# Token-major projection loop written out, two projections ahead of the turns, with the index scores inside it

## The chip, the cores and the metric

One Trainium2 chip, one of its cores. The metric is the device time of the whole program in microseconds (us), the median of three runs.

## The reference

A two-layer decoder trunk over 1024 positions of width 1024, in float32. Layer 0 has a gated short convolution beside a sparse attention, layer 1 a spatial gating unit beside a chunked linear attention, and each layer ends in a gated convolutional FFN. The change concerns the front of the sparse attention in layer 0:

```python
p = h @ w_in                                   # h: rmsnorm of x
sc, q, k, v, iq, ik, iw = split(p)             # 8 heads of q, one k, one v, 4 index heads iq, one ik, 4 weights iw
q = rope(rmsnorm(q, q_g)); k = rope(rmsnorm(k, k_g)); iq = rope(iq); ik = rope(ik)
isc = relu(einsum('bqhd,bsd->bhqs', iq, ik))   # index scores, 4 heads
isc = einsum('bhqs,bqh->bqs', isc, iw * IDX_SCALE)
idx = top_k(causal(isc), 256)                  # per query
out = softmax(q . k[idx] * ATT_SCALE) @ v[idx] # per query, on the chosen keys
```

## The kernel before

The residual stream lies transposed in SBUF (`xT`, 128 rows of features by 1024 tokens, eight of them). Matmul operands are split into a high and a low float16 part and multiplied in three passes. Each engine has its own queue, written out by hand, and waits on counting semaphores; nothing but these queues and semaphores sets the order.

The stage in question handles eight blocks (`NB`) of 128 tokens, "token-major": tokens lie on the partitions.

- **Projection** (PE, `tm_project`, matmuls at L1218): 964 columns (q, k, v, iq, ik, iw), eight steps of depth 128, six matmuls each, into the pair of PSUM banks 0/1 or 2/3 by the block's parity. A pair is free once ACT has copied the block two back (`tm_copied`).
- **Copy** (ACT, `tm_copy`, L1438): the pair to `tm` in SBUF, unscaled.
- **Norm and rotation** (DVE, `tm_block`, L1942 to L1960): squares of q and k, their sum over each head (L1943), ACT's Sqrt of it (`tm_rms`, L1442), reciprocal, two multiplications over 576 columns, the rotation of q and k and then of iq and ik by four short operations each, the high and low part of v, the scaled index weights. Each operation waits for the one before by a semaphore.
- **Parts** (ACT `tm_hi`, L1451 to L1453; DVE `tm_lo`, L1966 to L1968): high and low float16 parts of all rotated heads, into `tm_split`.
- **Turn** (PE, `tm_turn`, L1229): sixteen transposes into banks 4 and 5. It waits for the low parts of its block and for both evictions of the turn before.
- **Eviction** (ACT `tm_evict`, L1458: q; DVE, L1972: iq and keys).

PE's order: projections 0 and 1 (with a turn of convolution vectors between them, which DVE scales in `conv_vectors`, L1854 and L1855, behind block 0), turn 0, then in a loop of three bodies projection 2, turn 1, projection 3, turn 2 and so on, last turn 7. So a projection stands between two turns, one block ahead. While block 0 is on DVE, POOL splits the first two weight units of the next section.

**Index scores** follow, once all evictions are done: for blocks 2 to 7 and four heads each, PE multiplies the block's iq with all keys up to the block's end (L1259, `L = 128 (b + 1)` columns, two passes, four pairs of banks in turn), ACT applies relu into one of two rows (L1487), DVE multiplies by the token's weight and sums the four heads in `score[b]` (L2000 for the first head, L2004 for the others). Blocks 0 and 1 need no scores.

**What follows.** PE projects the convolution mixer in twelve units (`ev_sc`, L890). Meanwhile ACT (L1509) and DVE (L2035, L2077, L2083) search each query's 256th score by 31 halvings; single operations of the convolution mixer (L2163 first) are laid in between, each waiting for its unit. The attention begins when the search ends. Output projection, FFN, layer 1 and its FFN follow on PE.

**Memory.** One large tensor, `arena`, holds what lives for a stage. `tw_hi` and `tw_lo`, the split weights of the projection, lie at word 9600 and 13456, `tm` and `tm_split` at 17312 and 21536, the scores at 8736 to 13344, so over `tw_hi`. Six of the eight raw weight rows are loaded by SP to 17312 and up and split by POOL (L757, L760).

Of the kernel before, what the change touches and what calls it, by code (L numbers as in the profile page):

```python
# [64 lines left out]
TM_STEPS = 15  # L65
# [27 lines left out]
def build(nc, t, out, stop=None):  # L93
    ctx = ExitStack()
    with ctx:
# [62 lines left out]
        rope_c = view(8736, [NB, ROT])  # L158
        rope_s = view(8864, [NB, ROT])
        qk_gain = view(8992, [NH_NORM * HD])  # L160
# [4 lines left out]
        sq9 = view(19752, [NH_NORM * HD])  # L165
        rot_a = view(20328, [NH_NORM, ROT])
        rot_b = view(20472, [NH_NORM, ROT])
        rms9 = view(20616, [2, 16])
# [5 lines left out]
        TW_RAW = [None, None] + [17312 + EV_TM * i for i in range(KT - 2)]  # L174
# [12 lines left out]
        relu_buf = att  # L187
# [624 lines left out]
        def _(pe):  # L812
# [391 lines left out]
            def tm_project(b, par, wait):  # L1204
                if wait is not None:
                    pe.wait_ge(tm_copied, wait)
                for k in range(KT):
                    if par == 0 and wait is None:
# [6 lines left out]
                    for a, w in ((h_hi, tw_hi), (h_hi, tw_lo), (h_lo, tw_hi)):  # L1215
                        lhs = a[:, k, bass.ds(b * P, P)]
# [3 lines left out]
                last.then_inc(tm_done, 1)  # L1220

            def tm_turn(par, made, evicted):

                pe.wait_ge(tm_low, made)
                if evicted is not None:
                    pe.wait_ge(tm_evict_act, evicted)
                    pe.wait_ge(tm_evict_dve, evicted)
                for j in range(16):
                    last = tr(ps[:, 4 + j // 8, :].bitcast(F16)[:, j % 8 * P:(j % 8 + 1) * P], tm_split[:, par, j, :],  # L1229
                              ident16[:])  # L1230
                last.then_inc(tm_turned, 1)

            tm_project(0, 0, None)
# [17 lines left out]
            pe.wait_ge(tm_evict_dve, NB)  # L1251
            for b in range(2, NB):
                L = P * (b + 1)
                for h in range(IH):
                    if b >= 3:
                        pe.wait_ge(relu_ready, IH * (b - 3) + h + 1)
                    for c in range(0, L, HALF):
                        for rows in (ik_hh, ik_ll):
                            last = mm(pair(h)[:, c:min(L, c + HALF)], iq_st[:, h, b * P:(b + 1) * P],  # L1259
                                      rows[:, c:min(L, c + HALF)], start=(rows is ik_hh), stop=(rows is ik_ll))  # L1260
                    last.then_inc(idx_done, 1)


# [87 lines left out]
        def _(act):  # L1351
            A = nc.scalar.activation

            def after_register_wait():
                act.sem_inc(act_passed, 1)
# [78 lines left out]
            def tm_copy(par, done, free):  # L1434
                act.wait_ge(tm_done, done)
                if free is not None:
                    act.wait_ge(tm_low, free)
                A(tm[:, par, :], pair(par)[:, 0:EV_TM], ACT.Copy, scale=W_UNSCALE).then_inc(tm_copied, 1)  # L1438

            def tm_rms(par, b1):  # L1440
# [4 lines left out]
            def tm_hi(par, roped, turned):  # L1445
                act.wait_ge(tm_roped, roped)
                if turned is not None:
                    act.wait_ge(tm_turned, turned)
# [1113 lines left out]
```

## Time and profile before

| what | value |
|---|---|
| median of three runs | 2339.06 us (2338.33 to 2340.55) |
| the profiled execution, whole | 2339.65 us |
| its span, first to last instruction | 2337.8 us |
| mean granted clock of TensorE over the span | 0.952 |
| PE, DVE, ACT, POOL busy | 92%, 56%, 40%, 47% |

A profile lists each instruction with its start and duration. "Idle before" is the time in which its engine had nothing to do ahead of it, and what released it. A granted clock of 1.00 is TensorE's full speed. Times in the section of rows are microseconds from the start of the span, mean durations of a group nanoseconds.

### The profile page before, as it was taken

To read this page: it belongs to the slowest core of one execution; us is meant where nothing else is said; L and a number is where in the kernel's file an instruction comes from. 1 tells how busy PE (TensorE), PEld (TensorE's weight loads), DVE (VectorE), ACT (ScalarE), POOL (GpSimd) and SP (SyncE) were. 2 spreads that over 40 slices of the span, in tenths; PEclk is the share of its full clock that TensorE was granted. 3 is DMA by queue.
4 is the path that set the end of the run, shared out by engine and by line. 5 is a ranking of instruction groups with operands and counts; after the bars stand their busy time and mean duration, and the time that the engine had idled before them with its cause. 6 is when DMAs were issued, how large, how long until landed. Compare 5 with 4: busy or idle time off the path is not lost. (4 is left out here: it accounts for less than half of the span.)

```text
span 2337.8 us, 29990 instructions
## 1 busy us (share of the span) xinstructions
PE 2140.0 (92%) x11534; PEld 1044.8 (45%) x11534; DVE 1298.5 (56%) x1979; ACT 936.3 (40%) x1361; POOL 1098.9 (47%) x729
## 2 busy tenths in 40 slices
PE   7779927889999999999989999779999999999998
PEld 3434415644434444444434444464444444444444
DVE  9778888843876147514644023785577416631652
ACT  5247866621553045304413221651355215521530
POOL 5103304214784667456586022013488457745642
PEclk8989969999999999999999999769899999999999
DMA  4001200001112112111132001001111211211112
GB/s 163 18 0 37 55 0 1 20 19 58 32 54 72 39 52 72 54 54 55 48 103 70 2 28 37 10 20 54 36 37 56 71 54 48 61 54 54 55 34 92
DMA packets 185984, 109.79 MB, mean 47 GB/s; under 512 B 3871, under 2 KB 180422, under 8 KB 185878
## 3 DMA queue, kind: packets, MB, share of 16 engines
q1 hardware_dynamic: 185414, 107.00, 15.7%
q0 software_dynamic: 464, 1.39, 0.2%
q8 instruction: 65, 1.06, 0.2%
q14 instruction: 41, 0.34, 0.0%
HBM read 104.18 MB, written 4.19 MB: 46 GB/s over the span
## 5 line engine op out<-in xcount | busy, mean ns | idle before, releaser
L626 POOL TENSOR_SCALAR w_scaled<-stage 128x1024 f32<-128x1024 f32 (+1 forms) x100 | 108.0, 1080 | 840.5 <-PE ps L890 530.8
L969 PE MATMUL ps<-h_hi,arena 128*128 128x512 f16 x1280 | 391.3, 381 | 10.8 <-DVE arena L2291 6.5
L890 PE MATMUL ps<-arena,w_hi 128*128 128x512 f16 x1504 | 388.2, 381 | 10.2 <-POOL w_lo L629 7.7
L969 PE MATMUL ps<-arena 128*128 128x512 f16 x1440 | 317.3, 379 | 0.1
L2247 DVE SCALAR_TENSOR_TENSOR xT<-ps,xT 128x1024 f32 (+1 forms) x64 | 78.3, 1224 | 409.4 <-PE ps L890 362.5
L969 PE MATMUL ps<-h_lo,arena 128*128 128x512 f16 x640 | 243.7, 381 | 0.0
L2300 DVE SCALAR_TENSOR_TENSOR work<-ps,fvec,work 128x1023 f32<-128x1023 f32 (+1 forms) x176 | 221.4, 1278 | 25.3 <-ACT work L1590 22.2
L890 PEld LDWEIGHTS ps<-arena,w_hi 128*128 128x128 f16 x1504 | 147.0, 98 | 191.0 <-POOL w_lo L629 11.1
L890 PE MATMUL ps<-arena,w_lo 128*128 128x512 f16 x752 | 224.6, 380 | 0.0
L969 PEld LDWEIGHTS ps<-arena 128*128 128x128 f16 x1440 | 140.8, 98 | 170.2 <-POOL arena L701 0.6
L969 PEld LDWEIGHTS ps<-h_hi,arena 128*128 128x128 f16 x1280 | 125.7, 98 | 165.5 <-issue 14.7
L629 POOL TENSOR_TENSOR w_lo<-w_scaled,w_hi 128x1024 f16<-128x1024 f32 (+1 forms) x92 | 188.7, 2051 | 7.7
L1590 ACT ACTIVATE work<-ps,fvec 128x1024 f32<-128x1024 f32 x88 | 105.1, 1201 | 196.1 <-DVE ps L2291 196.1
L1369 ACT ACTIVATE stage<-stage 128x2048 f32<-128x2048 f32 x36 | 68.7, 1909 | 215.8 <-DMA stage<-in_ffn_w_up_dram 215.8
L2310 DVE TENSOR_TENSOR work<-work 128x1024 f32<-128x1024 f32 x44 | 102.9, 2338 | 28.0 <-ACT work L1595 28.0
L1509 ACT ACTIVATE stat<-arena,srch 128x1024 f16<-128x1024 f32 (+1 forms) x124 | 113.9, 921 | 10.8 <-DVE srch L2068 10.2
L695 POOL TENSOR_TENSOR arena<-arena 128x1024 f16<-128x1024 f32 x40 | 116.9, 2922 | 0.0
L683 POOL TENSOR_TENSOR arena<-stage,arena 128x1024 f16<-128x1024 f32 x36 | 83.0, 2305 | 67.6 <-ACT arena L1388 67.6
L890 PEld LDWEIGHTS ps<-arena,w_lo 128*128 128x128 f16 x752 | 73.8, 98 | 89.4 <-issue 1.1
L2291 DVE TENSOR_TENSOR ps<-stat,ps 128x512 f32<-128x512 f32 x80 | 55.7, 696 | 104.1 <-PE ps L969 99.6
L890 PE MATMUL ps<-h_hi,w_hi 128*128 128x512 f16 x352 | 106.6, 385 | 5.3 <-ACT arena L1487 4.2
L890 PE MATMUL ps<-h_lo,w_hi 128*128 128x512 f16 x352 | 106.2, 384 | 0.0
(363 smaller groups left out, 3754.4 us busy)
## 6 DMA issues: line engine op xcount, KB each, us to landing
stage<-in_ffn_w_up_dram SPq DMA_DIRECT2D x76, 512.0 KB, 4.5
stage<-in_ffn_w_down_dram SPq DMA_DIRECT2D x32, 512.0 KB, 4.0
stage<-in_od_w_in_dram SPq DMA_DIRECT2D x20, 512.0 KB, 3.7
stage<-in_ev_w_in_dram SPq DMA_DIRECT2D x12, 512.0 KB, 3.7
arena<-in_ffn_w_up_dram SPq DMA_DIRECT2D x12, 512.0 KB, 5.0
stage<-in_ffn_w_down_dram SPq DMA_DIRECT2D x16, 384.0 KB, 3.4
arena<-in_x_dram SPq DMA_DIRECT2D x8, 512.0 KB, 7.8
stage<-in_ev_w_out_dram SPq DMA_DIRECT2D x8, 512.0 KB, 3.9
```

The lines of the kernel that those rows point to most:

```text
L626: nc.gpsimd.tensor_scalar(scaled, src, W_SCALE, 1.0, ALU.mult, ALU.mult).then_inc(w_parts, 1)
L629: nc.gpsimd.tensor_tensor(lo, scaled, hi, ALU.subtract).then_inc(w_split, 1)
L683: G.tensor_tensor(lo[:, 0:1024], raw_of(layer, f, 0), hi[:, 0:1024], ALU.subtract)
L695: G.tensor_tensor(lo[:, 2560:3584], sums_b.rearrange("p s c -> p (s c)"), hi[:, 2560:3584], ALU.subtract).then_inc(su_split, 1)
L890: last = mm(out2[:, hf * HALF:(hf + 1) * HALF], w, a[:, k0 + k, hf * HALF:(hf + 1) * HALF], start=(first and k == 0 and pss == 0), stop=(l ...
L969: last = mm(ps[:, bank, :], left, right[:, k, :], start=(fresh and k == 0 and pss == 0), stop=(k == 3 and pss == 2), skip_group_check=True)
L1369: A(raw_pair(layer, f), raw_pair(layer, f), ACT.Copy, scale=W_SCALE).then_inc(su_scaled, 1)
L1509: return A(signs[c - len(BY_DVE)], score[b][:], ACT.Sign, bias=srch[:, S_CAND, c:c + 1], accum_out=srch[:, S_COUNT, c:c + 1])
L1590: A(work[:, 2 * fi + g, :], pair(2 * fi + g), ACT.Identity, bias=fvec[:, layer, f + (6 + g) * FT:f + (6 + g) * FT + 1], scale=fvec[:, laye ...
L2247: V.scalar_tensor_tensor(out=xT[:, m, :], in0=pair(pair0 + step * mi), scalar=W_UNSCALE, in1=xT[:, m, :], op0=ALU.mult, op1=ALU.add).then_ ...
L2300: V.scalar_tensor_tensor(out=acc[:, s:], in0=y[:, 0:T - s], scalar=fvec[:, layer, tap:tap + 1], in1=acc[:, s:], op0=ALU.mult, op1=ALU.add) ...
L2310: V.tensor_tensor(work[:, 2 * fi + 1, :], work[:, 2 * fi, :], work[:, 2 * fi + 1, :], ALU.mult).then_inc(hid_f, 1)
```

## The change

- PE does projections 0, 1 and 2 before turn 0; from then on projection b stands ahead of turn b - 2. The loops on PE, ACT and DVE are written out.
- The index scores of block b are issued within the loop. The four heads of blocks 2, 3 and 4 stand behind steps 4 to 7 of projections 5, 6 and 7. Blocks 5 to 7 are mixed with turns 6 and 7 and follow them. ACT's relus and DVE's sums stand in their queues in matching places. They use banks 6 and 7 singly for blocks 2 and 3 and the pairs 6/7 and 0/1 by turns from block 4 on; the relu rows are the two rows of `stat`.
- Squares, the high part of v and the index weights are made by ACT from PSUM, ahead of its copy. DVE's three multiplications of the rotation of both groups stand first, then both sums; most waits between its operations are gone (`TM_STEPS` 5 for 15). `conv_vectors` stands behind the sum of squares of block 0.
- `tw_hi` and `tw_lo` move to 13344 and up, clear of the scores; `tm` and `tm_split` move to `work`; tables, `sq9`, `qk_gain` and six raw rows move within `arena`.

The diff, cut to its core:

```diff
-        tw_hi = view(9600, [KT, EV_TM], F16)
-        tw_lo = view(9600 + 3856, [KT, EV_TM], F16)
-        tm = view(17312, [2, EV_TM])
-        tm_split = view(21536, [2, 16, 2 * HD], F16)
+        tw_hi = view(13344, [KT, EV_TM], F16)
+        tw_lo = view(13344 + 3856, [KT, EV_TM], F16)
+        tm = work[:, 0:2, 0:EV_TM]
+        tm_split = work[:, 2:4, :].bitcast(F16).rearrange("p a (j c) -> p a j c", c=2 * HD)
-        TW_RAW = [None, None] + [17312 + EV_TM * i for i in range(KT - 2)]
+        TW_RAW = [None, None, 21056] + [8352 + EV_TM * i for i in range(KT - 3)]
-        relu_buf = att
+        relu_buf = stat
...
+            def index_head(b, h):
+                n = IH * (b - 2) + h
+                L = P * (b + 1)
+                if h == 0:
+                    pe.wait_ge(tm_evict_dve, b + 1)
+                if n >= 2:
+                    pe.wait_ge(relu_ready, n - 1)
+                if b < 4:
+                    dst = ps[:, 6 + h % 2, :]
+                else:
+                    dst = pair(3 if h % 2 == 0 else 0)
+                    if h == 1:
+                        pe.wait_ge(tm_copied, 7)
+                    if (b, h) == (4, 0):
+                        pe.wait_ge(relu_ready, n)
+                for c in range(0, L, HALF):
+                    for rows in (ik_hh, ik_ll):
+                        last = mm(dst[:, c:min(L, c + HALF)], iq_st[:, h, b * P:(b + 1) * P],
+                                  rows[:, c:min(L, c + HALF)], start=(rows is ik_hh), stop=(rows is ik_ll))
+                last.then_inc(idx_done, 1)
...
-            tm_project(1, 1, None)
+            tm_project(1)
+            tm_project(2)
             pe.wait_ge(vec_ready, 2)
-            tm_turn(0, 1, None)
+            tm_turn(0)
             wait_half(0, 1)
-            with pe.Fori(0, 3) as i:
-                tm_project(i * 2 + 2, 0, i * 2 + 1)
-                tm_turn(1, i * 2 + 2, i * 2 + 1)
-                tm_project(i * 2 + 3, 1, i * 2 + 2)
-                tm_turn(0, i * 2 + 3, i * 2 + 2)
-            tm_turn(1, 8, 7)
+            for b in range(3, NB):
+                tm_project(b, b - 3 if b >= 5 else None)
+                tm_turn(b - 2)
+            index_head(5, 0)
+            index_head(5, 1)
+            tm_turn(6)
+            index_head(5, 2)
+            index_head(5, 3)
+            index_head(6, 0)
+            tm_turn(7)
+            for h in range(1, IH):
+                index_head(6, h)
+            for h in range(IH):
+                index_head(7, h)
...
+            def tm_copy(b):
+                act.wait_ge(tm_done, b + 1)
+                if b >= 1:
+                    act.wait_ge(tm_step, TM_STEPS * (b - 1) + 1)
+                src = pair(b % 2)
+                A(sq9[:], src[:, 0:NH_NORM * HD], ACT.Square, scale=W_UNSCALE)
+                A(v_hi[:, b, :], src[:, V0:V0 + HD], ACT.Copy, scale=W_UNSCALE)
+                A(iw_tok[:, b, :], src[:, IW0:IW0 + IH], ACT.Copy, scale=W_UNSCALE * IDX_SCALE)
+                if b >= 2:
+                    act.wait_ge(tm_low, b - 1)
+                A(tm[:, b % 2, :], src[:, 0:EV_TM], ACT.Copy, scale=W_UNSCALE).then_inc(tm_copied, 1)
...
+            for b in range(NB):
+                tm_copy(b)
+                tm_rms(b)
+                if b >= 2:
+                    tm_evict(b - 2)
+                if b >= 4:
+                    relu(b - 2, 0, 1)
+                tm_hi(b)
+                if b == NB - 1:
+                    tm_evict(NB - 2)
+                if b >= 4:
+                    relu(b - 2, 2, 3)
+            relu(NB - 2, 0)
+            tm_evict(NB - 1)
+            relu(NB - 2, 1, 2, 3)
+            relu(NB - 1, 0, 1, 2, 3)
...
+            for b in range(NB):
+                tm_sum(b)
+                if b == 0:
+                    conv_vectors()
+                if b >= 2:
+                    tm_evict(b - 2)
+                tm_rotate(b)
+                if b == NB - 1:
+                    tm_evict(NB - 2)
+                if b >= 4:
+                    add_index(b - 2, 0)
+                tm_lo(b)
+                if b >= 4:
+                    add_index(b - 2, 1, 2, 3)
+            tm_evict(NB - 1)
+            for b in (NB - 2, NB - 1):
+                add_index(b, 0, 1, 2, 3)
```

`relu(b, *heads)` and `add_index(b, *heads)` are the former loops over heads as functions. `tm_sum` is the reduce of `sq9`, `tm_rotate` the rest of the former `tm_block`.

## Rows read from the trace of the kernel before

**Rows 1.** The page: span and section 1, busy time of each engine.

```profile
PE 2140.0 (92%) x11534; PEld 1044.8 (45%) x11534; DVE 1298.5 (56%) x1979; ACT 936.3 (40%) x1361; POOL 1098.9 (47%) x729
```

**Rows 2.** Windows by stretch: busy time of each engine, granted clock, DMA.

```profile
83.90:138.70 54.80, 53.35 (x306) 26.46 (x303) 39.24 (x100) 16.90 (x31) 0.00 (x0) 1.00 0.00 0
138.70:149.70 11.00, 1.07 (x16) 0.90 (x16) 7.84 (x20) 3.17 (x6) 0.00 (x0) 0.67 0.00 0
149.70:152.80 3.10, 1.89 (x16) 1.63 (x16) 0.69 (x1) 1.02 (x1) 0.00 (x0) 0.50 0.00 0
152.80:160.00 7.20, 7.03 (x32) 3.29 (x32) 4.92 (x8) 4.99 (x9) 0.00 (x0) 0.77 0.01 2
160.00:176.40 16.40, 10.65 (x48) 3.88 (x48) 14.07 (x16) 12.81 (x17) 0.00 (x0) 1.00 0.00 0
...
178.00:302.00 124.00, 124.00 (x571) 56.04 (x570) 106.72 (x467) 101.56 (x210) 44.33 (x30) 0.99 0.16 43
302.00:333.00 31.00, 1.22 (x7) 0.44 (x5) 25.75 (x112) 26.46 (x53) 0.00 (x0) 0.57 0.00 0
```

**Rows 3.** Timeline of PE, 290 to 345 us: the first scores of the attention.

```profile
327.97 0.61 PE L1282 MATMUL ps<-arena 128*128 128x128 f16 x4 [25.36 <-DVE work L2176]
```

**Rows 4.** Timeline of DVE: scores of the last block; first convolution product.

```profile
172.62 0.75 DVE L2000 TENSOR_SCALAR arena<-arena 128x1024 f32<-128x1024 f32 x1
173.85 4.06 DVE L2004 SCALAR_TENSOR_TENSOR arena<-arena 128x1024 f32<-128x1024 f32 x3 [0.49 <-ACT arena L1487]
...
202.43 1.22 DVE L2163 SCALAR_TENSOR_TENSOR work<-ps,work 128x1024 f32<-128x1024 f32 x1
```

**Rows 5.** Timeline of PE, 50 to 200 us: start, duration, instruction, idle before.

```profile
70.48 1.89 PE L1229 MATMUL ps<-ident,arena 128*128 128x128 f16 x16 [11.81 <-DVE fvec L1855]
...
83.85 0.98 PE L1218 MATMUL ps<-arena,h_hi 128*128 128x512 f16 x4
...
92.41 0.98 PE L1218 MATMUL ps<-arena,h_hi 128*128 128x512 f16 x4
...
138.74 1.07 PE L1229 MATMUL ps<-ident,arena 128*128 128x128 f16 x16 [0.34 <-DVE arena L1968]
149.73 1.89 PE L1229 MATMUL ps<-ident,arena 128*128 128x128 f16 x16 [9.92 <-DVE arena L1968]
...
176.44 0.92 PE L890 MATMUL ps<-h_hi,w_hi 128*128 128x512 f16 x2 [4.15 <-ACT arena L1487]
```

**Rows 6.** Timeline of DVE in block 0, beside POOL's splitting of weights.

```profile
58.87 2.11 DVE L1953 TENSOR_TENSOR arena<-arena 128x144 f32<-128x144 f32 x1
...
63.16 2.25 DVE L1956 TENSOR_TENSOR arena<-arena 128x144 f32<-128x144 f32 x1
```

**Rows 7.** Groups of instructions by line and shape, 84 to 178 us: mean ns.

```profile
L1458 ACT ACTIVATE arena<-ps 128x1024 f16 x6 | 6.1, 1013 | 0.0
L1438 ACT ACTIVATE arena<-ps 128x964 f32<-128x964 f32 x6 | 5.8, 973 | 11.0 <-PE ps L1218 8.1 <-DVE arena L1968 2.9
...
L1946 DVE TENSOR_TENSOR arena<-arena 128x576 f32<-128x576 f32 x6 | 4.5, 758 | 0.2
...
L1966 DVE TENSOR_TENSOR arena<-arena 128x512 f16<-128x512 f32 x6 | 4.2, 692 | 3.7 <-ACT arena L1453 3.7
L1972 DVE COPY arena<-ps 128x1024 f16 x6 | 4.1, 692 | 0.0
...
L2004 DVE SCALAR_TENSOR_TENSOR arena<-arena 128x896 f32<-128x896 f32 x3 | 3.5, 1152 | 0.6 <-ACT arena L1487 0.4
...
L1487 ACT ACTIVATE arena<-ps 128x640 f32<-128x640 f32 x4 | 2.7, 702 | 0.8 <-DVE arena L2004 0.6 <-PE ps L1259 0.3
...
L1442 ACT ACTIVATE arena<-small,eps 128x9 f32<-128x9 f32 x6 | 1.8, 304 | 9.7 <-DVE small L1943 9.7
```

**Rows 8.** The later line that alternates Square (L1772) with Sqrt.

```profile
L1776 ACT ACTIVATE gla_rms<-gla_rms,eps x4: 300/301/302, 1571.6 to 1582.7; 128x8 f32<-128x8 f32 x4
L1776 ACT ACT_TABLE_LOAD  x1: 1283/1283/1283, 1570.3 to 1570.3; - x1
```

More of the change, by code:

```diff
@@ L1202, in _, with tm_project @@
             spread(0)
-            def tm_project(b, par, wait):
-                if wait is not None:
-                    pe.wait_ge(tm_copied, wait)
+            def index_head(b, h):
[18 more added lines that the diff above has]
+                last.then_inc(idx_done, 1)
+            def tm_project(b, index=None):
+                par = b % 2
+                if b >= 2:
+                    pe.wait_ge(tm_copied, b - 1)
                 for k in range(KT):
-                    if par == 0 and wait is None:
+                    if b == 0:
                         wait_tile(0, 0, k)
@@ L1219, in tm_project, with tm_turn @@
                                       start=(k == 0 and a is h_hi and w is tw_hi), stop=(k == KT - 1 and a is h_lo))
[L1220 to L1227, printed above, removed]
+                    if k == KT - 1:
+                        last.then_inc(tm_done, 1)
+                    if index is not None and k >= KT - IH:
+                        index_head(index, k - (KT - IH))
+            def tm_turn(b):
+                pe.wait_ge(tm_low, b + 1)
+                if b:
+                    pe.wait_ge(tm_evict_act, b)
+                    pe.wait_ge(tm_evict_dve, b)
                 for j in range(16):
-                    last = tr(ps[:, 4 + j // 8, :].bitcast(F16)[:, j % 8 * P:(j % 8 + 1) * P], tm_split[:, par, j, :],
+                    last = tr(ps[:, 4 + j // 8, :].bitcast(F16)[:, j % 8 * P:(j % 8 + 1) * P], tm_split[:, b % 2, j, :],
                               ident16[:])
                 last.then_inc(tm_turned, 1)
-            tm_project(0, 0, None)
+            tm_project(0)
             pe.wait_ge(small_landed, 16 * 8)
@@ L1486, in _ @@
                         act.wait_ge(idx_added, n - 1)
[L1487 removed]
+                    src = ps[:, 6 + h % 2, :] if b < 4 else pair(3 if h % 2 == 0 else 0)
+                    A(relu_buf[:, n % 2, 0:L], src[:, 0:L], ACT.Relu).then_inc(relu_ready, 1)
+            for b in range(NB):
+                tm_copy(b)
+                tm_rms(b)
+                if b >= 2:
+                    tm_evict(b - 2)
[10 more added lines that the diff above has]
+            relu(NB - 1, 0, 1, 2, 3)
             A(small[:, 60:61], eps[:, 0:1], ACT.Copy).then_inc(a_cg, 1)
@@ L1947, in tm_block @@
+                st(V.reciprocal(rms9[:, b % 2, 0:9], rms9[:, b % 2, 0:9]))
+                st(V.tensor_tensor(heads, heads, rms9[:, b % 2, 0:9].unsqueeze(2).broadcast_to([P, 9, HD]), ALU.mult))
                 st(V.tensor_tensor(cur[:, 0:n9], cur[:, 0:n9], qk_gain[:], ALU.mult))
-                for c0, nh in ((Q0, 9), (IQ0, 5)):
+                groups = [(Q0, 0, NH_NORM), (IQ0, NH_NORM, IH + 1)]
+                for c0, r0, nh in groups:
                     g = cur[:, c0:c0 + nh * HD].rearrange("p (h d) -> p h d", d=HD)
+                    ra, rb = rot_a[:, r0:r0 + nh, :], rot_b[:, r0:r0 + nh, :]
@@ new lines, in tm_rotate @@
+                    V.tensor_tensor(rb[:, :, 0:8], g[:, :, 8:16], tab(rope_s, 0, 8), ALU.mult)
+                    last = V.tensor_tensor(rb[:, :, 8:16], g[:, :, 0:8], tab(rope_s, 8, 16), ALU.mult)
+                st(last)
+                for c0, r0, nh in groups:
+                    g = cur[:, c0:c0 + nh * HD].rearrange("p (h d) -> p h d", d=HD)
+                    V.tensor_tensor(g[:, :, 0:16], rot_a[:, r0:r0 + nh, :], rot_b[:, r0:r0 + nh, :], ALU.add)
+                V.tensor_tensor(v_lo[:, b, :], cur[:, V0:V0 + HD], v_hi[:, b, :], ALU.subtract).then_inc(tm_roped, 1)
```

139 lines of the change are left out of this document (42 added, 97 removed).

## The prediction

> **What bounds the kernel now.** The page says PE is busy for 92% of the span [rows 1], an average that says nothing of the stage the change touches. So I read the first 333 us stretch by stretch, in the windows [rows 2]. From 83.9 to 138.7 us PE does five projections and works nearly all the time. From 138.7 to 152.8 it works 3 us of 14. From 152.8 to 176.4 come the index scores; PE works 18 of 24 us, DVE 19. From 178 to 302 PE projects the convolution mixer without a gap, DVE and ACT search for the top keys. From 302 to 333 PE is idle for all but 1.2 us and the search still runs: the attention starts when the search ends, and PE's wait of 25.36 us there is for DVE [rows 3]. The search starts when the last index score is summed, at 177.91 us [rows 4]. So one moment sets all that follows: the end of the last sum. Whatever it gains, the attention gains.
>
> Which wait comes last ahead of it? PE's timeline [rows 5] shows three. PE stands 11.81 us before the turn of block 0, as DVE finishes that block late: beside POOL's splitting of weights, operations of DVE that take 0.3 us in later blocks take 2.11 and 2.25 us [rows 6]. PE stands 9.92 us before the turn of block 7, as no projection is left to lay over that block's chain. And only then do the index scores begin.
>
> **Part by part.** Durations are those of [rows 7] unless another group is named. I lay the new order out by hand on three queues, with 0.05 to 0.1 us for each semaphore.
>
> *Two projections ahead of the turn.* Block 0's chain on DVE keeps its start, since POOL's splits stay where they are. It loses the square (0.76 us), the cast and the scaling, but DVE now turns the convolution vectors in front of the rotation (0.8 us) and still meets POOL. I get it rotated at 66.8 us and its low part done at 69.5, against 69.7 before. PE has projection 2 to do meanwhile (58.6 to 68.4), so it waits 1.2 us in place of 11.81. Turn 0 ends at 70.5 and projection 3 starts there; ACT's copy of block 1, which it needs, ends at 69.9. Before, it started at 83.85 [rows 5]. **Gain 13.3 us.**
>
> *Projections 3 to 7.* The eight steps of a projection start 1.223 us apart (83.85 to 92.41 in seven [rows 5]), so 9.8 us; a turn takes 0.9 us of PE. Five projections and turns 1 to 4 are 52.5 us. New inside projections 5 to 7 are the twelve heads of index blocks 2 to 4: 8 x (384 + 512 + 640) columns at 1.223/2892 us make 5.2 us, and 0.6 us for their starts. Turn 1 waits 0.3 us for ACT's eviction of block 0, queued behind the copy of block 2. Together 58.7 us, so turn 5 starts at 129.2. Before, turn 6 stood in that place, 54.9 us after the start of projection 3 [rows 5]. **Loss 3.8 us.**
>
> Does the ACT-DVE chain keep up? For a block that carries heads it is: copy with Square and two small copies, reduce 0.75, DVE's eviction 0.69, reciprocal to low part of v 3.9 (two multiplications of 0.76, six small ones, three sums, no waits between those), then ACT's parts 1.25 once its relus of two heads are done, DVE's parts 1.4, one sum, one relu, next copy. ACT's new work is unseen. Square of 576 columns from PSUM lies under the relu of 640 (0.70) and above one of 384 (0.49); I take 0.68. The small copies lie under the 0.30 of the 9-element Sqrt; I take 0.25 and 0.20. With the copy (0.97) that is 1.85 us, against 0.97. The chain comes to 12 us a block, PE's cycle to 12.2, 12.6 and 13.2. The first head of each block finds its keys evicted 1.5 to 2.5 us early. With 0.95, 0.30 and 0.25 the end is 1.5 us later; with 0.50, 0.20 and 0.15 it is 0.7 us earlier.
>
> *The tail.* ACT's copy of block 7 stands behind the relu of index block 4, head 3, and ends at 132.4 instead of 131. Reduce, eviction of block 5 (133.9), rotation to 137.8, eviction of block 6, first sum of index block 5, low part to 140.6. Then DVE is nearly always at work: three sums of 1.02 us and their waits (to 143.8), eviction of block 7 and the first sum of block 6 (145.1), a wait of 0.6 us for ACT's relu, three sums of 1.15 (149.2), and for block 7 what it takes today, 5.3 us (172.62 to 177.91 [rows 4]). The last sum ends at 154.4, 25.3 us after turn 5; before it ended 39.2 us after turn 6. **Gain 13.9 us.** Sum: 13.3 - 3.8 + 13.9 = 23.4 us.
>
> *The clock.* In the stretches where PE worked 1 of 11 and 1.9 of 3.1 us, the granted clock was 0.67 and 0.50, so at the lower level (1.2 GHz) for much or all of them; it was 0.77 in the next 7 us, and 1.00 from 160 us on with PE busy for 65% [rows 2]. The new tail leaves PE two holes of 4 and 3 us, at 130 and 137.5, so some heads will run at 1.2 GHz. If all of blocks 5 to 7 did, a head's matmuls and relu, with two pairs of banks to alternate between and not four, would take over from DVE as the limit: end at 158.6, 4.2 us later. From the rows I allow a quarter, 1.1 us. **Net gain 22.3 us.**
>
> *Costed at nothing.* The parts, tables and weights in other rows: the same eight loads on SP's queue in the same order, nothing moved past another; the rope tables wait for POOL's first split, which the first projection needs as well. Loops written out: five projections and turns of 9.8 and 0.9 us fill 53.5 of the 54.8 us of their window [rows 2], so the branches and waits they hold cost at most 0.3 us a block. No DMA and no POOL work is added; POOL's splits and SP's loads of the next section wait for PE's units and shift with them. The relu rows now lie where ACT writes its signs, but those wait for the search, after the last sum. PE's convolution section starts at the last relu, 1.6 us before the last sum, as today, so its lead over the search stays. After the search everything waits on other engines, none on a fixed time; the shift goes through whole.
>
> *A rule against it.* ACT now alternates Square, Copy and Relu with Sqrt, eight times. In the later line that alternates four groups of Squares with four Sqrts, one table load of 1.28 us stands before the first Sqrt and none before the others [rows 8]; so none here. The Trainium skill (ScalarE: Activation LUTs, Table sets: the hidden batching unit) says functions in different sets cost a load at each switch, and names copy and relu, not Square, among those in every set. By that reading this would be two loads a block; the row speaks against it, and by the row the sum stays.
>
> **The rivals.** (a) *The clock holds the tail down*: 4.2 us lost, 2339.1 - 19.2 = 2319.9. For it: 0.50 at 150 us. Against: 1.00 at 65% load. (b) *Table loads*: 2 x 1.28 us on ACT for blocks 1 to 7. Laid out, projection 7 ends 4.7 us later and the last sum at 161.2: 2322.3. (c) *Lockstep, slower than before*: ACT stands for head 1 in front of its parts, head 1 stands in the second half of a projection, and that projection waits for ACT's copy two blocks back. If these lock, blocks 5 to 7 pay one after another: PE's 13.2 plus the chain's 12, 25 us, against 12.7. That is 37 us more: 2354. It turns slower than before from 20 us a block on. Against: each wait reaches one block further back than the lock needs. (d) *Nothing arrives*: the search's end is held by something else, or the search slows by what was gained. The first convolution product in the search, at 202.4 us [rows 4], needs PE's second unit, due two units of 10.3 us (124/12) and a slow first 2.3 us after 176.4: a cover of 3 us. But both shift together: 2339.
>
> **The numbers.** The sum is made against the profiled execution: 2339.65 us, of which 2337.8 are the span and 1.85 lie around it and stay. 2339.65 - 22.3 = 2317.4; it lies 0.6 above the median of the runs, 2339.06, so the median should come to 2316.8. Chances: forecast 0.68, (a) 0.16, (b) 0.04, (c) 0.04, (d) 0.03, and 0.05 for a chain that is longer without locking (up to 2330). The unknown costs give 2315 (short ACT work, no cold clock) to 2321 (long ACT work, rival a). The clock's phase at later stage starts moves by the shift, an estimate of 2 us either way from the 3 us that stretches at 0.77 and 0.50 lose here. So 2312 to 2325. A measurement of this kernel tells about 0.2%, 4.7 us, from no change. Faster by more than that: 0.68 + 0.16 + 0.04 + 0.05 = 0.93; within: 0.03; slower: 0.04.
>
> **What would show it.** Right: PE's wait before the turn of block 0 near 1 us; projection 3 starts near 70.5; turn 5 near 129; the last sum near 155.5; the convolution section still 124 us; PE's wait before the attention still 25 us. Wrong: table loads between Sqrt and Square; heads inside projections that wait for evictions or relus by more than 1 us; blocks 5 to 7 longer than 14 us; a granted clock near 0.5 from 140 to 155; a stage after the search with another length than before.

## The result, and the profile after

The changed kernel takes 2311.94 us (median of 4 runs, 2310.62 to 2315.07); the kernel before, measured beside it, 2339.56 us (2338.33 to 2340.55). The ratio is 0.9887 with a 95% interval of 0.9875 to 0.9898: 27.6 us less, where 22.3 were forecast. The median lies 0.06 us below the lower end of the predicted range; those of two repeats below, 2314.21 and 2312.97, lie inside it. The profiled execution has a span of 2310.9 us against 2337.8, so 26.9 us less.

The page after, where [rows 1] was read before. PE's share is the same 92% and its busy time fell by 12.6 us, so 14.3 of the 26.9 us are idle time that went. The matmuls are the same 11534, and the mean granted clock rose from 0.952 to 0.958:

```profile
PE 2127.4 (92%) x11534; PEld 1037.7 (45%) x11534; DVE 1286.1 (56%) x1955; ACT 940.6 (41%) x1385; POOL 1098.9 (48%) x729
```

Windows of the changed kernel, for [rows 2] (columns: the stretch, its length, then the busy time of PE, PEld, DVE, ACT and POOL, the granted clock, the DMA share and GB/s):

```profile
69.40:127.10 57.70, 57.70 (x339) 29.69 (x337) 39.75 (x110) 27.66 (x60) 0.00 (x0) 1.00 0.00 1
127.10:134.00 6.90, 3.43 (x27) 1.98 (x25) 6.14 (x13) 4.32 (x8) 0.00 (x0) 0.77 0.01 2
134.00:138.10 4.10, 2.57 (x27) 1.76 (x26) 3.66 (x12) 3.55 (x6) 0.00 (x0) 0.97 0.00 0
138.10:150.10 12.00, 8.49 (x48) 3.40 (x48) 10.50 (x11) 9.26 (x11) 0.00 (x0) 1.00 0.00 1
150.10:154.00 3.90, 3.86 (x18) 1.79 (x19) 3.49 (x14) 0.00 (x0) 0.00 (x0) 1.00 0.00 0
...
274.20:304.30 30.10, 0.42 (x2) 0.00 (x0) 24.42 (x106) 26.36 (x56) 0.00 (x0) 0.56 0.00 1
```

From 69.4 to 127.1 us PE has no idle time at all: five projections with twelve heads in them. The stretch with 1 us of work in 11 is gone; what is left of it are the 6.9 us from 127.1, with the clock at 0.77. After 134 us the clock is 0.97 to 1.00.

PE's timeline of the changed kernel, for [rows 5] and [rows 3] (start, duration, instruction, in brackets the idle time before it and what ended it):

```profile
68.46 1.05 PE L1255 MATMUL ps<-ident,work 128*128 128x128 f16 x16 [0.79 <-DVE work L2004]
69.35 0.98 PE L1241 MATMUL ps<-arena,h_hi 128*128 128x512 f16 x4
...
127.06 1.06 PE L1255 MATMUL ps<-ident,work 128*128 128x128 f16 x16
...
131.59 2.74 PE L1222 MATMUL ps<-arena 128*128 128x512 f16 x8 [3.47 <-DVE arena L2008]
...
138.06 0.92 PE L1222 MATMUL ps<-arena 128*128 128x512 f16 x4 [1.53 <-ACT stat L1498]
...
150.14 0.59 PE L890 MATMUL ps<-h_hi,w_hi 128*128 128x512 f16 x2 [1.69 <-ACT small L1519]
...
304.34 0.61 PE L1305 MATMUL ps<-arena 128*128 128x128 f16 x4 [29.73 <-DVE work L2211]
```

Turn 0 waits 0.79 us instead of 11.81, and projection 3 begins 14.50 us earlier. Turn 5 (127.06) takes the place of turn 6 before (138.74). The last row is the surprise: the attention begins 23.6 us earlier, but PE's wait ahead of it has grown from 25.36 to 29.73 us. The convolution section, which starts at 150.14, gained 26.3 us, and the search that runs beside it gained less.

DVE's timeline of the changed kernel, for [rows 4] and [rows 6], and then what follows the last sum:

```profile
58.56 2.12 DVE L1988 TENSOR_TENSOR arena<-work,arena 128x144 f32<-128x144 f32 x1
...
62.87 2.14 DVE L1990 TENSOR_TENSOR arena<-work,arena 128x40 f32<-128x40 f32 x1
...
146.16 0.75 DVE L2017 TENSOR_SCALAR arena<-stat,arena 128x1024 f32<-128x1024 f32 x1
147.39 4.06 DVE L2021 SCALAR_TENSOR_TENSOR arena<-stat,arena 128x1024 f32<-128x1024 f32 x3 [0.48 <-ACT stat L1498]
...
160.16 6.01 DVE L2087 TENSOR_SCALAR work<-srch 128x6 int32<-128x6 int32 x31
166.20 0.22 DVE L2112 TENSOR_SCALAR srch<-srch 128x1 int32<-128x1 f32 x2
```

The last sum ends at 151.45 (147.39 + 4.06), 26.46 us earlier than before. Ahead of the search DVE makes a table of flipped bits, 31 short operations on six elements. DVE's timeline of the kernel before shows what they took there:

```profile
186.63 2.35 DVE L2052 TENSOR_SCALAR work<-srch 128x6 int32<-128x6 int32 x31
189.00 0.22 DVE L2077 TENSOR_SCALAR srch<-srch 128x1 int32<-128x1 f32 x2
```

They took 2.35 us, and now take 6.01. The search's first bit therefore starts 22.80 us earlier (189.00 to 166.20): 3.66 of the 26.46 us were given back in one place. POOL's timeline names the other party. The first row is of the kernel before:

```profile
188.94 1.04 POOL L626 TENSOR_SCALAR w_scaled<-stage 128x1024 f32<-128x1024 f32 x1 [123.69 <-PE ps L890]
```

and these are of the changed kernel:

```profile
160.95 1.09 POOL L626 TENSOR_SCALAR w_scaled<-stage 128x1024 f32<-128x1024 f32 x1 [95.99 <-PE ps L890]
162.00 1.04 POOL L627 TENSOR_SCALAR w_hi<-stage 128x1024 f16<-128x1024 f32 x1
163.13 2.15 POOL L629 TENSOR_TENSOR w_lo<-w_scaled,w_hi 128x1024 f16<-128x1024 f32 x1
```

POOL splits weights of the convolution section as soon as PE's first unit releases their buffer. Before, that unit began with the clock at 0.57, as a window of the kernel before shows:

```profile
176.40:180.40 4.00, 3.96 (x11) 1.53 (x12) 3.55 (x15) 0.00 (x0) 0.00 (x0) 0.57 0.00 0
```

It took 12.5 us to POOL's start, and POOL began as the flips ended (188.94 against 188.98). Now PE begins the unit at full clock, POOL starts 10.81 us after it, and its three operations (4.33 us) lie inside the flips. The Trainium skill (SBUF — State Buffer, Who interferes with whom) says that VectorE and GpSimd share one pair of ports as an exclusive lock, that a VectorE operation with two inputs in SBUF contends for it with a GpSimd instruction that reads SBUF, and so does a `tensor_scalar` in a two-port form, where the loser stands for the whole instruction. The rows agree in the times: 3.66 us are lost over 4.33 us of POOL, and in block 0 an operation that takes 0.31 us in later blocks takes 2.12 and ends at 60.68, where POOL's subtraction ends at 60.52. Which form the flips take, no row shows.

ACT's timeline of the changed kernel, the table load of block 0 and then block 5, for the prices taken by estimate and for [rows 8]:

```profile
54.09 1.28 ACT L1471 ACT_TABLE_LOAD   x1
...
102.93 0.65 ACT L1462 ACTIVATE arena<-ps 128x576 f32<-128x576 f32 x1
103.46 0.23 ACT L1463 ACTIVATE arena<-ps 128x64 f16<-128x64 f32 x1
103.56 0.20 ACT L1464 ACTIVATE arena<-ps 128x4 f32<-128x4 f32 x1
103.61 1.01 ACT L1467 ACTIVATE work<-ps 128x964 f32<-128x964 f32 x1
105.44 0.30 ACT L1471 ACTIVATE arena<-small,eps 128x9 f32<-128x9 f32 x1 [0.82 <-DVE small L1962]
```

This table load stands before the first Sqrt, and none follows in the seven blocks after it.

### The profile page after: what moved, and what is told of

It reads as the page before. It is cut to its first block and busy times, and to the rows that moved or that the text cites. A ratio compares the mean times of both kernels' runs of the same rounds, so it can differ in the third digit from the quotient of the medians.

```text
span 2310.9 us, 29711 instructions
## 1 busy us (share of the span) xinstructions
PE 2127.4 (92%) x11534; PEld 1037.7 (45%) x11534; DVE 1286.1 (56%) x1955; ACT 940.6 (41%) x1385; POOL 1098.9 (48%) x729
## 5 line engine op out<-in xcount | busy, mean ns | idle before, releaser
L969 PE MATMUL ps<-h_hi,arena 128*128 128x512 f16 x1280 | 391.3, 381 | 11.6 <-DVE arena L2326 6.5
L2335 DVE SCALAR_TENSOR_TENSOR work<-ps,fvec,work 128x1023 f32<-128x1023 f32 (+1 forms) x176 | 221.4, 1278 | 26.5 <-ACT work L1619 23.4
L1585 ACT ACTIVATE work<-xT 128x1024 f32 (+1 forms) x24 | 25.4, 1057 | 201.5 <-DVE xT L2282 201.5
```

The lines of the kernel that those rows point to most:

```text
L969: last = mm(ps[:, bank, :], left, right[:, k, :], start=(fresh and k == 0 and pss == 0), stop=(k == 3 and pss == 2), skip_group_check=True)
L2335: V.scalar_tensor_tensor(out=acc[:, s:], in0=y[:, 0:T - s], scalar=fvec[:, layer, tap:tap + 1], in1=acc[:, s:], op0=ALU.mult, op1=ALU.add) ...
```

## The experiments

The first set was measured against 13 runs of the kernel before, 2338.94 us in the median. The question: which part of the change brings which part of the 26.5 us at the last sum, and does POOL cause the 3.7 us lost behind it?

**The index heads back behind the loop.** The second projection ahead stays; the relus and sums follow the heads, on four pairs of banks.

```diff
             for b in range(3, NB):
-                tm_project(b, b - 3 if b >= 5 else None)
+                tm_project(b)
                 tm_turn(b - 2)
...
             tm_turn(6)
...
             tm_turn(7)
...
+            pe.wait_ge(tm_evict_act, NB)
+            pe.wait_ge(tm_evict_dve, NB)
+            for b in range(2, NB):
+                for h in range(IH):
+                    index_head(b, h)
```

> The changed kernel with all index scores behind the loop again, on four pairs of banks as in the kernel before; two projections ahead and ACT's squares stay. My theory (each part is worth what it takes off the way to the last index sum): without heads the five projections and turns run at 10.7 us a block, turn 7 starts near 131, and the 25.1 us of index scores of the kernel before follow, so the last sum is near 158, 7 us later than in the changed kernel: 2319 us, give or take 2. Rival (DVE has the same number of sums to do either way, so hiding them in the loop brings nothing): last sum within 2 us of 151.5, 2312. Rival (the heads inside cost PE more than they save): below 2310.

Measured: 2321.53 us (2318.34 to 2323.68), ratio 0.9925 (0.9909 to 0.9942); the last sum at 159.78, 8.3 us later than in the changed kernel. PE's timeline of this kernel:

```profile
126.32 1.05 PE L1246 MATMUL ps<-ident,work 128*128 128x128 f16 x16 [2.98 <-ACT arena L1474]
...
131.64 1.89 PE L1246 MATMUL ps<-ident,work 128*128 128x128 f16 x16 [4.26 <-DVE work L1985]
134.64 7.14 PE L1213 MATMUL ps<-arena 128*128 128x384 f16 x32 [1.12 <-ACT arena L1474]
...
158.46 0.77 PE L890 MATMUL ps<-h_hi,w_hi 128*128 128x512 f16 x2 [4.31 <-ACT small L1500]
```

The holes before turns 6 and 7 (2.98 and 4.26 us) stay empty, and all heads come after them. Two more things can be read. PE's convolution section starts after a wait of 4.31 us, its first pair of matmuls takes 0.77 us instead of 0.59, POOL starts 12.50 us behind it instead of 10.81, and DVE's flips take 2.34 us: with the longer hole the collision is gone. And the span, 2319.9, is 9.0 us above that of the changed kernel, although the attention starts only 5.7 us later (310.02); the rest comes at later stage starts.

**One projection ahead as well.** The kernel above, with turn b - 1 behind projection b as in the kernel before; the evictions on ACT and DVE move with the turns. What is left of the change are the squares and small copies on ACT, the shorter rotation with fewer waits, the written-out loops and the new rows.

```diff
-            tm_project(2)
...
-            for b in range(3, NB):
+            for b in range(2, NB):
                 tm_project(b)
-                tm_turn(b - 2)
-            tm_turn(6)
+                tm_turn(b - 1)
```

> As the run with the index scores behind the loop, and also one projection ahead of the turn, as in the kernel before; what is left of the change is ACT's squares, the fewer waits on DVE and the other rows. My theory: turn 0 near 68, block time 10.7 us in place of 11.1, block 7's chain 9 us in place of 11, last sum near 170, 8 us before that of the kernel before: 2331 us. So the second projection ahead is worth 12 us, the index scores inside 7, the rest 8. Rival (the lighter operations of DVE carry the change, two ahead only moves the wait): under 2320. Rival (they carry nothing): 2338 or more.

Measured: 2333.6 us (2331.38 to 2337.98), ratio 0.9978 (0.9969 to 0.9988); the last sum at 172.03. PE's timeline of this kernel:

```profile
69.00 1.87 PE L1246 MATMUL ps<-ident,work 128*128 128x128 f16 x16 [11.28 <-DVE work L1982]
...
143.86 1.89 PE L1246 MATMUL ps<-ident,work 128*128 128x128 f16 x16 [8.16 <-DVE work L1982]
```

Both long holes are back: 11.28 us before turn 0, 8.16 before turn 7. The last sum now has its parts: 177.91 before, 172.03 with the lighter block (5.9 us), 159.78 with a second projection ahead (12.3), 151.45 with the heads inside (8.3). The expectation had named 8, 12 and 7 for them. Each is larger by itself than the 4.7 us that a measurement tells from no change, and the whole kernel's times are in the same order (2339, 2334, 2322, 2312). They were taken off in this one order only, so what each would bring without the others is not shown.

**The squares back on DVE.** ACT loses the Square, DVE gets a multiplication of 576 columns per block.

```diff
-                A(sq9[:], src[:, 0:NH_NORM * HD], ACT.Square, scale=W_UNSCALE)
...
+                V.tensor_tensor(sq9[:], qk, qk, ALU.mult).then_inc(tm_step, 1)
```

> The changed kernel with the squares of q and k on DVE again (from the copied row, with a wait before the reduce). My theory: in the blocks of the loop PE is the limit and hides 0.3 us of a longer chain; only block 0 and the tail show it, last sum 0.3 to 1 us later, 2312 to 2313 us, no change that can be measured. Rival (the chain of ACT and DVE sets the block): 0.3 to 0.8 us in each of seven blocks, last sum 2 to 5 us later, 2314 to 2317.

Measured: 2314.98 us (2313.82 to 2317.07), ratio 0.9897 (0.9881 to 0.9914). Turns 0 to 5 start within 0.08 us of the changed kernel's, the first head of block 5 at 131.91 instead of 131.59, and the last sum at 152.58, 1.1 us later (the two repeats below, at 151.57 and 151.06, lie 1.0 and 1.5 us ahead of it). So inside the loop PE sets the pace and either engine may square; in the tail DVE does, and the multiplication costs there. The change of the total lies inside the spread of runs.

**POOL waits for the flips.** One wait before POOL's split for the third unit, for a semaphore that reaches 2 only when the flips are done.

```diff
-            split_section("ev_sc", 6, 2, peeled=6)
+            split_section("ev_sc", 6, 2, peeled=6, after_two=lambda: pool.wait_ge(cand_ready, 2))
```

> The changed kernel; POOL holds its split of the third unit of the convolution section until DVE has written the 31 flip rows ahead of the search (6.0 us in the changed kernel, 2.35 before). My theory (the flips met POOL's split, and POOL held DVE up): the flips take 2.4 us again, the search starts 3.7 us earlier, PE waits under 1 us for the third unit, and the end comes 2.5 to 4 us earlier, 2308 to 2309.5 us, apart from 2 us either way by the clock. Rival (the flips are slow for another reason, such as where they lie): they stay at 6 us and the time stays at 2312. Rival (PE then waits for POOL's late unit and the search meets that): the section of PE grows by 4 us and the time stays or grows.

Measured: 2310.97 us (2307.81 to 2313.08), ratio 0.9885 (0.9868 to 0.9901), profiled span 2306.0. DVE's timeline of this kernel, the flips:

```profile
159.21 2.34 DVE L2087 TENSOR_SCALAR work<-srch 128x6 int32<-128x6 int32 x31
```

and PE's, the start of the attention:

```profile
299.05 0.61 PE L1305 MATMUL ps<-arena 128*128 128x128 f16 x4 [25.38 <-DVE work L2211]
```

The flips take 2.34 us again, PE's wait before the attention is 25.38 us as before ([rows 3]: 25.36), and the attention begins 28.9 us earlier than before instead of 23.6. Of the 5.3 us between them, 0.95 lie ahead of the last sum (150.50), where the edit changes nothing. The last sum to the attention takes 148.55 us against 152.89: 3.67 of these 4.34 us are the flips, the other 0.67 stand in the search behind them. Keeping POOL away is the only difference, so POOL's splits are shown as the cause of what the search lost. In the median of the runs the gain is smaller than in the span (1 us, across two sets of measurements), and by the total alone it would not be shown.

The second set (before: 2339.22 us) repeats the changed kernel and asks three things: how far two profiles of one kernel differ, whether the meeting with POOL depends on the clock, and what POOL costs in block 0.

**The changed kernel again**, without an edit.

> The changed kernel once more, for a second profiled execution and beside the next runs. My theory on the 3.3 us that the first profile gained behind the search (PE's stage starts met another phase of the clock): last index sum again 26 to 27 us ahead of the kernel before, flips again 6 us, and the shift behind the search between 22 and 28 us, not steady at 27: it moves by 1 to 3 us at 360 to 390 us and at 1640 to 1740 us. Time 2310 to 2315. Rival (something in the change speeds the later stages): the same 3.3 us at the same places.

Measured: 2314.21 us (2311.46 to 2315.02), ratio 0.9888 (0.9872 to 0.9905). Last sum 151.57, flips 6.03 us, attention at 304.45: the same to 0.12 us. But the output projection behind the attention starts at 468.05, where the first profile has 466.42, and the span is 2311.8. So 1.6 us of the first profile's lead at that place are not the change's.

**A delay of 0.9 us in the tail.**

```diff
             for b in (NB - 2, NB - 1):
+                if b == NB - 1:
+                    for _ in range(1):
+                        V.memset(work[:, 3, :], 0.0)
                 add_index(b, 0, 1, 2, 3)
```

> The changed kernel with one write of 1024 columns of zeros on DVE between index blocks 6 and 7, nothing else: everything behind it is put off by that time, about 0.6 to 1 us. My theory (what follows the last sum is rigid apart from the clock and the meeting of POOL with the flips): last sum 0.6 to 1 us later, flips still near 6 us, time 1 us more, give or take 2. Rival (the flips' meeting is a matter of a fraction of a us): flips change by over 1 us.

Measured: 2315.41 us (2314.35 to 2316.12), ratio 0.9894 (0.9878 to 0.9911). The last sum ends at 152.86, 1.4 us later (0.45 of them stand already at turn 0, ahead of the edit), yet the attention begins at 303.08, 1.3 us earlier than in the changed kernel. The theory missed and its rival came true. DVE's timeline of this kernel, the memset and the flips:

```profile
147.24 0.91 DVE L2042 MEMSET work<- 128x1024 f32 x1 [0.16 <-issue]
...
161.57 2.34 DVE L2090 TENSOR_SCALAR work<-srch 128x6 int32<-128x6 int32 x31
...
164.57 0.87 DVE L2073 TENSOR_SCALAR_CACHE_REDUCE arena<-arena,srch 128x640 uint8<-128x640 f32 x1
```

POOL's timeline and a window of the same kernel:

```profile
164.05 1.04 POOL L626 TENSOR_SCALAR w_scaled<-stage 128x1024 f32<-128x1024 f32 x1 [98.64 <-PE ps L890]
```

```profile
149.50:154.00 4.50, 2.45 (x9) 1.05 (x10) 3.98 (x10) 1.43 (x3) 0.00 (x0) 0.85 0.00 2
```

PE's hole before the section grew from 1.69 to 2.27 us, the clock there fell from 1.00 to 0.85, and POOL started 12.50 us after the section instead of 10.81, just behind the flips. A delay of 0.9 us removed a collision of 3.7. By the end the lead is gone: the span is 2313.8 us against 2310.9 and 2311.8, as this profile gains nothing at the later stage starts (see below). The rows also show what doesn't suffer: the comparison with a running count beside POOL's split (164.57) takes 0.87 us, as it does without POOL.

**The kernel before, POOL after block 0's rotation.** How much of PE's 11.81 us in the kernel before was POOL's doing?

```diff
             norm_lows(0)
+            pool.wait_ge(tm_roped, 1)
             split_section("ev_sc", 6, 2, peeled=6)
```

> The kernel before, but POOL holds its first two splits of the convolution section until block 0 is rotated. My theory (POOL held DVE up in block 0): the rotation of block 0 takes 5.5 us in place of 11, turn 0 is at 61 to 62 us in place of 70.5, and all that follows is 8 to 9 us earlier: 2330 us. So of the 13.3 us that I put down to the second projection ahead, 9 could be had without it. Rival (DVE was slow by its own chain of waits): turn 0 stays at 70, 2339.

Measured: 2335.9 us (2335.3 to 2337.06), ratio 0.9985 (0.9976 to 0.9995). A miss: turn 0 starts at 66.94, not at 61 to 62. DVE's timeline of this kernel:

```profile
57.07 0.31 DVE L1954 TENSOR_TENSOR arena<-arena 128x144 f32<-128x144 f32 x1
...
61.27 1.51 DVE L1967 TENSOR_TENSOR arena<-arena 128x512 f16<-128x512 f32 x1 [1.31 <-ACT arena L1454]
62.70 2.33 DVE L1968 TENSOR_TENSOR arena<-arena 128x256 f16<-128x256 f32 x1
64.96 1.29 DVE L1969 TENSOR_TENSOR arena<-arena 128x256 f16<-128x256 f32 x1
```

The rotation now takes its 0.31 us, and the three operations of the low part, which POOL's splits have been moved onto, take 5.1 us instead of 1.5. The last sum ends at 174.62, 3.3 us earlier than before.

**The changed kernel, POOL clear of the rotation and of the flips.** Both waits together.

> The changed kernel with both meetings of POOL and DVE taken away: POOL's first two splits wait for block 0's rotation, the third for the flips. My theory: turn 0 follows projection 2 without a wait, at 67.5 to 68 us, 0.5 us gained at most since projection 2 covered the rest; flips 2.35 us, 3.7 us gained; last sum near 151, the attention 4 to 5 us earlier, 2307 to 2309. Rival (a chain of ACT and DVE limits blocks 1 and 2, so an early block 0 brings more): last sum 2 us or more earlier, 2305.

Measured: 2310.55 us (2307.48 to 2311.45), ratio 0.9871 (0.9855 to 0.9888); turn 0 at 67.34, last sum 150.72, attention at 299.25, span 2308.6. The last sum to the attention takes 148.53 us, so the wait for the flips brings what it brought alone. What the one for the rotation brings is small and not clear of the scatter: turn 0 starts at 67.82 to 68.46 in the three profiles of the changed kernel.

The third set (before: 2339.01 us) moves POOL one step further and looks for the fastest version.

**The kernel before, POOL after block 0's low part**, `pool.wait_ge(tm_low, 1)` in the same place.

> The kernel before, but POOL holds its first two splits until block 0's low parts are made, not only until it is rotated (there the three low-part operations took the blow: 1.5, 2.3 and 1.3 us in place of 0.7, 0.4 and 0.4). My theory (POOL held DVE up wherever it met an operation with two inputs in SBUF): low parts done at 62.7, turn 0 at 63.5, 7 us earlier than before; all that follows 7 us earlier: 2332 us. Rival (the blow falls on block 1 then, which nothing hides): turn 1 and later ones 2 to 4 us late, 2335.

Measured: 2335.36 us (2332.97 to 2337.92), ratio 0.9985 (0.9975 to 0.9995). Turn 0 starts at 62.77, 7.7 us earlier than before. But DVE's timeline of this kernel shows block 1 paying:

```profile
65.44 2.25 DVE L1947 TENSOR_TENSOR arena<-arena 128x576 f32<-128x576 f32 x1
...
70.29 2.11 DVE L1955 TENSOR_TENSOR arena<-arena 128x72 f32<-128x72 f32 x1
```

Turn 1 then waits 1.95 us (77.45), and the last sum at 172.72 is 5.2 us earlier. In both places where POOL's 9 us of splits were put, the next operations of DVE carried them, and 5.2 us at the last sum is the most that moving them brought. The second projection ahead hides nearly all of that in block 0, and brings 12.3.

**The changed kernel, POOL clear, evictions first.** Both waits (for block 0's low part and for the flips), and in the loop DVE evicts block b - 2 before it sums the squares of block b.

```diff
+                if b >= 2:
+                    tm_evict(b - 2)
                 tm_sum(b)
                 if b == 0:
                     conv_vectors()
-                if b >= 2:
-                    tm_evict(b - 2)
```

> The changed kernel with POOL's first splits behind block 0's low parts, its third behind the flips, and DVE's eviction of block b - 2 in front of the sum of squares of block b, where DVE waits for ACT's copy anyway. My theory: turn 0 at 67.3, flips 2.35 us, the chain of each block 0.6 us shorter, which PE hides up to block 7 and the tail shows: first head of index block 5 0.6 to 1.2 us earlier, last sum near 149.8 to 150.3; 2306 to 2309 us, the fastest of all. Rival (turns come later than DVE's sum and DVE now waits for them): last sum 151 or later.

Measured: 2309.08 us (2307.32 to 2311.14), ratio 0.9873 (0.9857 to 0.9890): the fastest kernel of the study. PE's timeline of this kernel:

```profile
128.66 2.65 PE L1223 MATMUL ps<-arena 128*128 128x512 f16 x8 [2.27 <-DVE arena L2009]
...
297.96 0.61 PE L1306 MATMUL ps<-arena 128*128 128x128 f16 x4 [25.38 <-DVE work L2212]
```

Turn 0 starts at 66.36 and the first head of block 5 at 128.66. That is 2.9 us earlier than in the changed kernel. From turn 0 to that head it takes 62.30 us against 63.13 in all three profiles of the changed kernel, so 0.8 come from the eviction, which no longer stands behind the reduction; the rest, 2.1 us by the first profile and 1.5 by the third, is the earlier turn 0. The last sum ends at 149.42, and the attention starts 30.0 us earlier than before.

**The changed kernel a third time**, beside the one above.

> The changed kernel again, beside the run with POOL out of the way and the eviction first: last sum near 151.5, flips near 6 us, 2312 to 2315 us; the other run should be 4 to 6 us below it. If the shift behind the search is again another at 360 to 390 or at 1640 to 1740 us, it is the clock's and not the change's.

Measured: 2312.97 us (2312.68 to 2315.22), ratio 0.9890 (0.9874 to 0.9907); last sum 151.06, attention at 303.95, output projection at 466.59, span 2310.8. All its runs lie above all of the kernel shown just before (2307.32 to 2311.14), which is 3.9 us faster by the medians; the intervals of the two ratios overlap all the same.

## Why the prediction was right, and where it wasn't

**What bounds the kernel: right in the main.** The end of the last sum sets the search, the search sets the attention. The kernel before, the two that take the change apart, and the changed kernel order themselves by it. To a fraction of a microsecond it is not so. In the six profiles whose section starts at a low clock, the attention begins 139.02 to 139.06 us after POOL begins the split of the third unit, while the last sum ends 11.03 to 11.61 us ahead of that split. So a last sum that comes 0.6 us earlier against POOL moves nothing. The tap operations of the convolution mixer, which DVE does within the search, level it out: beside POOL's later splits the eight of them take 12.3 us where the last sum leads by 11.03 and 12.9 where it leads by 11.61.

**Two projections ahead (13.3 us): 14.5.** Turn 0 was due at 69.6 with a wait of 1.2 us and came at 68.46 with 0.79. DVE met POOL again, as said, and the rotation still ended at 65.64, not at 66.8.

**Projections 3 to 7 (3.8 us lost): 2.8.** The eight steps and a turn take 10.7 us, and the three blocks with heads 11.97, 12.41 and 12.85 us against 12.2, 12.6 and 13.2. No head inside a projection waited. The prices by bounds held: Square 0.63 to 0.65 (0.68 taken), small copies 0.21 to 0.23 and 0.17 to 0.20 (0.25 and 0.20).

**The tail (13.9 us, less 1.1 for the clock): 14.8.** Turn 5 to the last sum takes 24.4 us, not 25.3, nor 26.4 with the clock. From reciprocal to low part of v DVE needs 3.4 us (131.44 to 134.87) and not 3.9. The clock was 0.77 from 127 to 134 and 0.97 to 1.00 from there on, with PE busy for 63 and 71% of the stretches from 134 and from 138; PE's holes of 3.47 and 1.53 us were shorter than the 4 and 3 laid out. Rival (a) is out: its loss of 4.2 us wasn't there. Together the last sum is 26.5 us earlier where 22.3 were forecast.

**"The shift goes through whole": wrong, and the step that failed.** It was costed at nothing that POOL's splits shift with PE's units. They shift with PE's clock too. PE's section was called "as today"; but in the kernel before it started after a wait of 4.15 us with the clock at 0.57, and now after 1.69 us with 1.00. That brought POOL onto the flips: 3.66 us given back. The thirteen profiles of this study agree. Where the wait was 1.69 us and nothing held POOL, it started 10.81 or 10.82 us after the section and the flips took 6.01 to 6.04 us (four profiles); where the wait was 2.27 to 4.31 us, it started 12.49 to 13.08 us after it and they took 2.34 or 2.35 (six); where POOL was held for the flips they took 2.34 (three). The wait itself is shorter since PE can no longer run ahead: with two pairs of banks the last head ends at 148.45, 3.0 us before the last sum, and with four it ended at 172.29, 5.6 us before. The run with the heads behind the loop has four pairs again, and 5.6 us. No run changes the banks alone. The sentence under "nothing arrives", that the search may slow by what was gained, named the kind of event but not its place, and its worked case (the convolution product at 202 us) was not the one. The rest of the search became 0.8 us shorter, so the attention gained 23.6. Of this, 0.7 lie in the eight tap operations, which meet POOL's later splits at other points: together they take 12.3 us before and 11.6 now (10.9 with POOL held for the flips). DVE's timeline shows the first pair, in the kernel before and then in the changed kernel:

```profile
212.35 3.98 DVE L2171 SCALAR_TENSOR_TENSOR work<-work,vec 128x1023 f32<-128x1023 f32 x2
```

```profile
189.43 2.60 DVE L2206 SCALAR_TENSOR_TENSOR work<-work,vec 128x1023 f32<-128x1023 f32 x2
```

Before, POOL's subtraction of that unit ran from 211.80 to 213.93, into the first of them; now one ends at 185.93, ahead of both.

**The clock's phase (2 us either way): 3.3 us in this profile.** Windows of the kernel before and of the changed kernel around the same stage start:

```profile
1669.00:1690.00 21.00, 17.61 (x56) 8.51 (x56) 15.27 (x22) 10.94 (x16) 10.94 (x7) 0.61 0.18 50
```

```profile
1643.40:1662.00 18.60, 14.88 (x56) 6.98 (x57) 14.16 (x20) 10.04 (x14) 10.76 (x7) 0.82 0.20 56
```

The same 56 matmuls run at a mean clock of 0.61 and 0.82. The gain of 1.6 us is in the first sixteen of them, in PE's timeline of the kernel before and then of the changed kernel:

```profile
1668.66 3.58 PE L846 MATMUL ps<-ones,work 128*128 128x1 f32 x16 [0.83 <-ACT work L1556]
```

```profile
1643.43 1.95 PE L846 MATMUL ps<-ones,work 128*128 128x1 f32 x16 [0.83 <-ACT work L1585]
```

1.5 more came in the attention; the second profile of the same changed kernel has 0.4 of it. The 1.6 stay in seven of the twelve other profiles, all three of the changed kernel among them; two have lost them again by 1800 us, and three never have them. So this part is a matter of the execution and of where the stage falls. What decides it was not found, and no run here could set it.

So the profile gained 26.9 us where 22.3 were forecast, by errors that partly cancel: the last sum 4.2 us better than forecast, 3.7 us given back at the flips, and some 3 us on top from later stage starts and 0.8 from the search. Rival (d) is out: the shift arrived. Rival (b) is shown false by ACT's rows. For this the Trainium skill's list of functions in every table set (ScalarE: Activation LUTs, Table sets: the hidden batching unit), read as if Square needed another set than Sqrt, would have been the wrong guide; the rows of one load for eight alternations decide. Rival (c), the lockstep, shows nowhere: PE had no wait between 69.4 and 127.1 us.

## What to carry to other kernels

When one engine waits for a chain of others once per block, lay a second block's work in front of the wait before polishing the chain: here it brought 12.3 us on top of the 5.9 that shortening the chain brought. Work that moves as a whole still meets other neighbours than before; list for each engine what starts on the release of another, and check whether a start of that other at a higher clock moves it onto a run of short operations. And take an interference away by a wait only with an eye on what is next in line: POOL's splits, pushed off one block, fell upon the next.

## What was not expected of the hardware

Thirty-one operations of VectorE on six elements take 2.34 us alone and 6.01 beside three operations of GpSimd on 1024 columns that last 4.33 us; the shortest operations suffer as much as the long ones. A hole of 1.69 us left PE's clock at 1.00 and one of 2.27 at 0.85 in the rows of two kernels that differ by one memset, and with that the first unit took 1.7 us longer until POOL's start, so that the later kernel was the earlier one at the attention. Three profiles of one program agree to 0.5 us at the last sum and at the attention (to 0.64 at turn 0) and differ by 1.6 us behind it. And the search on DVE fell into step with POOL's splits: in six profiles the attention follows POOL's split of the third unit by 139.02 to 139.06 us, although the last sum's lead over that split differs by 0.6 us.
